# Three 32-byte pads in front of the moving operands of the matmuls

## The reference

```python
for i in range(2):                                     # first_block
    x = x + 0.5 * swiglu(rms_norm(x, ln_ffn1[i]), ...) # d_ff = 2816
    h = rms_norm(x, ln_mix[i])
    x = x + even_mixer(h, ...) if i % 2 == 0 else x + odd_mixer(h, ...)
    x = x + 0.5 * swiglu(rms_norm(x, ln_ffn2[i]), ...)
    x = x + sigmoid(rms_norm(x, ln_ple[i]) @ ple_w_gate[i]) * (p[i] @ ple_w_in[i])
# second_block: one mixer of three branches (conv, RG-LRU, RWKV-7), then an MLP of width 4096
x = x + (gate_a * y_a + gate_b * y_b + gate_c * y_c) @ w_out
x = x + square(relu(rms_norm(x, norm2) @ w1)) @ w2
return rms_norm(x, final_g)
```

## The kernel before

| tensor | start | over a multiple of 64 | over a multiple of 256 |
|---|---|---|---|
| `x` | 16512 | 0 | 128 |
| `h` | 24704 | 0 | 128 |
| `raw` | 41088 | 0 | 128 |
| `w_hi` | 53376 | 0 | 128 |
| `w_lo` | 65664 | 0 | 128 |
| `a_hi` | 77952 | 0 | 128 |
| `a_lo` | 81024 | 0 | 128 |
| `arena` | 101120 | 0 | 0 |
| `h_of_feed_forward` | 133888 | 0 | 0 |

## Time and profile before

### The profile page before, as it was taken

The page is one execution under the profiler, slowest core; times in us unless marked ns, Lnnn a source line. Parts: engine busy times, 40 slices in busy tenths (PEclk is TensorE's granted clock), DMA queues, the critical chain, the costliest instruction groups (busy, mean ns, idle before and its releaser), DMA issues.

```text
span 1788.0 us, 38474 instructions
## 1 busy us (share of the span) xinstructions
PE 1717.7 (96%) x14874; PEld 1609.7 (90%) x14874; DVE 1295.5 (72%) x2130; ACT 992.0 (55%) x1543; POOL 2.5 (0%) x8
## 2 busy tenths in 40 slices
PE   7999899999999999998999999989999999889998
PEld 6999899899999989998988999989999998789997
DVE  6777767657777887777767777777787775567776
ACT  5445555445444564445555444568878875344443
POOL 0000000000000000000000000000000000000000
PEclk9999999899999999999999999999999999999999
DMA  6555443115555455554425565445555540145553
GB/s 233 187 177 189 140 140 107 60 49 180 184 181 188 154 165 179 187 186 136 148 79 175 188 188 177 159 159 181 175 188 178 177 154 4 63 130 183 184 184 118
DMA packets 75721, 277.74 MB, mean 155 GB/s; under 512 B 8416, under 2 KB 8672, under 8 KB 75104
## 3 DMA queue, kind: packets, MB, share of 16 engines
q1 hardware_dynamic: 75168, 273.58, 47.5%
q0 software_dynamic: 448, 2.62, 0.4%
HBM read 274.07 MB, written 2.10 MB: 154 GB/s over the span
## 4 chain that ended last, share of the span: by engine, by line
PE 89%; DVE 6%; ACT 3%; issue 1%; DMA 0%; DVEq 0%; SPq 0%; ACTq 0%
PE ps L461 87%; DVE w_lo L450 1%; PE ps L2270 1%; ACT w_hi L442 1%; DVE rstd L566 0%; DVE arena L634 0%; ACT arena L1938 0%; DVE rstd L624 0%; DVE h L533 0%; DMA x<-x_t 0%; DVE x L787 0%; DVE arena L757 0%; DVE arena L761 0%; ACT h L525 0%; DVE a_lo L777 0%
## 5 line engine op out<-in xcount | busy, mean ns | idle before, releaser
L461 PE MATMUL ps<-h,w_hi 128*128 128x256 f32 (+1 forms) x3460 | 756.2, 309 | 0.0
L450 DVE TENSOR_TENSOR w_lo<-raw,w_hi 128x1024 fp32r<-128x1024 f32 x514 | 623.3, 1214 | 104.6 <-ACT w_hi L442 95.2
L442 ACT ACTIVATE w_hi<-raw 128x1024 fp32r<-128x1024 f32 x514 | 538.8, 1050 | 235.6 <-PE ps L461 220.6
L461 PE MATMUL ps<-h,w_lo 128*128 128x256 f32 x2066 | 598.0, 290 | 28.5 <-DVE h L630 14.3
L461 PEld LDWEIGHTS ps<-h,w_hi 128*128 128x128 f32 x3460 | 572.4, 195 | 29.5
L461 PEld LDWEIGHTS ps<-h,w_lo 128*128 128x128 f32 x2066 | 401.9, 195 | 35.2 <-issue 21.4
L461 PE MATMUL ps<-h_of_feed_forward,w_hi 128*128 128x512 f32 (+1 forms) x1008 | 340.5, 383 | 0.0
L461 PE MATMUL ps<-a_hi,w_lo 128*128 128x256 f32 x1032 | 293.6, 285 | 8.8 <-DVE a_lo L777 8.8
L461 PE MATMUL ps<-a_hi,w_hi 128*128 128x256 f32 x1032 | 292.3, 283 | 0.0
L461 PE MATMUL ps<-a_lo,w_hi 128*128 128x256 f32 x1032 | 292.3, 283 | 0.0
L461 PE MATMUL ps<-h_of_feed_forward,w_lo 128*128 128x256 f32 x960 | 269.9, 283 | 0.6 <-issue 0.6
(11 more groups left out here) (327 smaller groups left out, 1226.0 us busy)
## 6 DMA issues: line engine op xcount, KB each, us to landing
raw<-weights SPq DMA_DIRECT2D x514, 512.0 KB, 3.4
con<-shape_constants SPq DMA_DIRECT2D x1, 1618.0 KB, 10.4
x<-x_t SPq DMA_DIRECT2D x1, 1024.0 KB, 4.9
stored<-x POOLq DMA_DIRECT2D x1, 1024.0 KB, 5.0
x<-stored POOLq DMA_DIRECT2D x1, 1024.0 KB, 7.9
out_t<-arena SPq DMA_DIRECT2D x4, 256.0 KB, 2.1
arena<-p_t POOLq DMA_DIRECT2D x2, 256.0 KB, 4.6
par<-parameters SPq DMA_DIRECT2D x1, 172.5 KB, 2.4
```

The source lines that it names most:

```text
L442: A.activation(w_hi[:, u % RING, 0:n], raw[:, u % RING, 0:n], ACT.Copy).then_inc(s_hi, 1)
L450: V.tensor_tensor(w_lo[:, u % RING, 0:n], raw[:, u % RING, 0:n], f(w_hi[:, u % RING, 0:n]), SUB)\
L461: return TE.matmul(o, lhsT, rhs, start=start, stop=stop, skip_group_check=True)
```

## The change

Three tensors of eight float32 columns (32 bytes in each partition) are allocated and never used. The first stands in front of `h`, the second behind it, the third in front of `a_hi`.

```diff
         x = sb("x", [P, KT, T])
+        sb("in_front_of_h", [P, 8])
         h = sbr("h", [P, KT, 2, T])
         h_hi, h_lo = h[:, :, 0, :], h[:, :, 1, :]
+        sb("behind_h", [P, 8])
         raw = sb("raw", [P, RING, UNIT])
         w_hi, w_lo = sbr("w_hi", [P, RING, UNIT]), sbr("w_lo", [P, RING, UNIT])
+        sb("in_front_of_a", [P, 8])
         a_hi, a_lo = sbr("a_hi", [P, 3, T]), sbr("a_lo", [P, 3, T])
```

## The result

The changed kernel takes 1770.98 us in the median (1769.08 to 1772.34), the kernel before 1788.87 on the same chip: ratio 0.9895, 95% interval 0.988 to 0.9911. That is 17.9 us less, where 39.9 were forecast. One execution of `apart_32`, a placement tried further down, took 4371.14 us for a reason that was not found, and it is left out of that kernel's median and ratio.

A forecast was written before the change was run, and what follows sets the result against it. TensorE, busy 96% of the span, was taken as the bound. 1788.0 - 41 for matmul spacing + 1 gave 1748.0 us of span, and with 0.9 us between span and median 1749 us; range 1675 to 1815.

The forecast's parts named there:

- the mechanism: In TensorE's fp32r matmuls at full clock, a surplus of 0.013 to 0.020 us each, read as limited operand reading from SBUF.
- The sign: In fp32r matmuls, moving operands standing apart from the weights stream faster; faster overall was given 0.50.
- The ceiling: All matmuls reading shifted moving operands, at one column per cycle: at most 151 us (8.4%) to gain.
- The first term, -41 us: Matmuls with shifted moving operands: 3.9 ns less each, 41 us in all, the geometric mean of 11 and 151.
- The lower measured price, 0.8% or 11 us: Low bound of the matmul gain, from ffn0 against ffn1: 2.8 ns a pair, 0.8% of 1450 us.
- That ffn0's pairs would gain as ffn1's: Pairs of 256 and 512 columns: ffn0 (0.354 us) and ffn1 (0.350) must show the same sign of change.
- The second mixer's 1 us for ScalarE's chain: Second mixer: its 9 us gain may run into waits for ScalarE, busy 80%, so 1 us is taken off.
- The other two effects, at 0: VectorE and ScalarE operands at new places, 0; DMAs of constants and stores beginning 32 bytes off, 0 up to +1 us.
- Nothing moves: Rival for all matmul streams: a unit of 32 bytes or less counts, or TensorE's own surplus; 1789 us, chance 0.22.
- Slower by an extra unit: Rival for every fp32r stream: one more 64-byte unit touched, 7.5 ns a matmul at most, 1793 to 1868 us, chance 0.28.
- The whole surplus goes: Rival for all matmuls: the two streams miss each other entirely, 151 us less in matmuls, 1646 us, chance 0.06.
- The 0.9 us between span and median: Whole kernel: added to the predicted span of 1748.0 us to give the median of 1749 us.

The follow-up runs named there:

- apart_32: Kernel before with 224 bytes behind `h` and 32 in front of `a` (differences to the weights 32, 32, 160): 1765.64 us, ratio 0.9886.
- all_32: Kernel before with one 32-byte pad in front of `h`, shifting moving tensors and weights alike: 1788.14 us, ratio 1.000.
- weights_32: Kernel before with 32-byte pads in front of `w_hi` and behind `w_lo`, shifting the weights instead: 1772.43 us, ratio 0.9911.
- the tables: Matmul-only kernels, whole computation left out, over differences between moving and weight starts: 113.3 to 123.5 ns per 256 columns with weights at 0.
- apart_192: Kernel before with small tensors moved and pads added, weights on a multiple of 256, differences 192, 192, 160: 1760.26 us, ratio 0.9853.
- fine_256: Matmul-only kernel, whole computation left out: 72 matmuls of 256 columns for each of 35 moving starts, mostly 8 bytes apart: 113.3 to 123.5 ns.
- apart_4: Kernel before with `h` and `a` starting 4 bytes over the weights' place modulo 256, `h_of_feed_forward` at 192: 1811.84 us, ratio 1.0142.

## Why the prediction was right or wrong

**What bounds the kernel, and the mechanism: right as far as it was tested.** The distance from start to start is what the change moved, VectorE's and ScalarE's durations stayed (w_lo's 1214 ns is 1214 after), and no wait took the gain away. That the distance between the moving operand and the weights is what counts was read from one comparison, `h` against `h_of_feed_forward`, and all_32 and weights_32 confirm it. The sign wasn't luck for 256 columns: no difference that is a multiple of 16 bytes took longer than 120.1 ns, and difference 0 takes 120. For pairs it was only a tendency (346.4 to 360.0 around 353.1). Why the difference counts, the limit in the reading of SBUF, stays a reading that no run shows.

**The ceiling: of no use as a scale.** 151 us assumed 106.7 ns for 256 columns. No run of 256 fp32r columns in 87 combinations went below 113.3, with any width of weights. Worked out from that lowest value and 346.7 for a pair, the ceiling is about 7278 x 6.6 + 672 x 6.6 + 912 x 4.4 = 56 us. The Trainium skill, "TensorE: Matmul & The Clock Gate", section "Wait — 56ns, not 53.3ns?", puts warm matmuls at N / 2.4 GHz plus about 2.5 ns, for 256 columns an estimate of 109.2 ns; the tables don't reach that either.

**The first term, -41 us: the step that failed.** The size was the geometric mean of 11 and 151, one measured price and one bound that is out of reach. It came to 3.9 ns a matmul, and it assumed one sign and size for all streams because all moved by 32 bytes. In fact they went to three different differences: `h` to 32 below the weights' place, `a` to 32 above it, `h_of_feed_forward` from 128 to 160. By the tables: 4182 matmuls of 256 columns against `h` from 119.9 to 118.3, 6.7 us; 3096 against `a` from 119.9 to 116.7 or 117.8, 6.5 to 9.9 us; 912 pairs of `h_of_feed_forward` from 351.1 to 346.6, 4.1 us; 672 pairs of `h`, nothing. That sums to 17 to 21 us for the measured 17.9; with the averages of the two traces (1.7 ns against `h`, 2.8 against `a`, 3.8 for a pair of `h_of_feed_forward`) it is 19. "0.116 or less" was named as what would confirm the forecast; the rows show 0.117 and 0.118. The lower measured price, 0.8% or 11 us, was nearer to the truth than the mean.

**That ffn0's pairs would gain as ffn1's: wrong** in the execution of the result, where 0.353 stayed at the difference 224. In the second profiled execution of the changed kernel they did gain (0.347) in ffn0 and not in ffn2, and no reasoning from addresses, the prediction's or that of the tables, foresaw this.

**The second mixer's 1 us for ScalarE's chain: right in place, not needed here.** In the changed kernel TensorE stands idle for 0.2 us of 260 there; in `apart_192`, with a larger gain per matmul, ScalarE enters the chain in exactly that stage, and the idle time there grows by about 1 us.

**The other two effects, at 0: right.** all_32 shifts `arena`, the constants and `a` for VectorE, ScalarE and the DMAs by 32 bytes and is level with before within 0.2%.

**The rivals.** *Nothing moves* rested on a unit of 32 bytes or less. It is out. A step of 16 bytes does show in fine_256: but for one, no start off a multiple of 16 took less than 120.0 ns. *Slower by an extra unit* didn't come, and all_32, in which every stream begins 32 over a multiple of 64, shows that there is no such price. A loss exists at another place: `apart_4` is 1.4% slower. *The whole surplus goes* was out of reach.

The 0.9 us between span and median was 1.8 in the changed kernel's runs (a run with a span of 1767.3 took 1769.08); it changes nothing here.

## What to carry to other kernels

Where TensorE runs fp32r matmuls back to back at the full clock, measure the distance from start to start against the columns over 2.4 GHz; if there is a surplus, the difference of the moving and the stationary start addresses is a free parameter (5.6% of a run of 256 columns between 0 and 192, 1.9% of this kernel), to be read from a table of a few hundred microseconds rather than guessed from one shift. Keep the moving start on a multiple of 16 bytes (the weights' start was never taken off one here), take the difference modulo 256 per stream (a tensor that serves two shapes of matmul can't have both optima), and check it in the kernel, in more than one execution, since the pattern depends on what ran before and differed between two executions of one kernel. When a price is bounded by one measured row and one ideal, stay near the row.

## What the runs showed of the hardware that was not expected

- Of two streams at the same pair of addresses modulo 256 the spacing can be one of several values, each exactly repeating: 353.3 or 346.7 ns a pair at difference 0, 113.3 or 117.8 at 192, by the stream that ran just before.
- The changed kernel, at one set of addresses, ran the pairs of ffn0 at 346.7 ns and those of ffn2 at 353.0 in one execution, and both at 352.9 in another.
- 113.3 ns was the lowest spacing seen for 256 fp32r columns, with 128, 64 or 32 columns of weights.
- 32 above the weights (116.7) and 32 below them (118.3) are not alike.
- A start 4 bytes over the weights' place costs 123.5 ns for 120.0, and 359.2 a pair for 353.3.
